# An ordered opening and five rearranged stage borders in a two-block transformer kernel on one Trainium2 core

## The chip, the core and the metric

The kernel runs on one core of a Trainium2 chip. The metric is the device time of one execution in microseconds (us). Times of one execution come from the hardware profiler. Engines are named as the profile names them: PE (TensorE, matrix products; PEld is its weight load), DVE (VectorE), ACT (ScalarE), POOL (GpSimd), SP (SyncE, which issues DMAs). A trailing q (SPq, ACTq) means the queue in which an engine issues.

## The reference

Two transformer blocks work on a batch of one, 512 tokens of width 1024, in fp32. The change touches the first block only:

```
x = x + 0.5 * swiglu(rms_norm(x, norm_ffn1_w), ffn1_w_in, ffn1_w_out)
x = x + hybrid_mixer(rms_norm(x, norm_mix_w), ...)      # SSD scan + differential attention
x = x + memory_cross_attention(rms_norm(x, norm_cross_w), rms_norm(mem, norm_mem_w), w_cq, w_ck, w_cv, w_co)
x = x + 0.5 * swiglu(rms_norm(x, norm_ffn2_w), ffn2_w_in, ffn2_w_out)
...
z, xbc, dt_raw, q, k, v = split_sizes(h @ w_in, IN_SIZES)   # in hybrid_mixer
y = ssd_scan(...) gated by silu(z), normed in 4 groups
logits = q k^T * scale + bias[rel_bucket], causal; w = p0 - lam * p1 ; o = w v, normed per head
return concatenate([y_ssd, y_attn]) @ w_out
```

There are 16 SSD heads of 64 in 4 groups, chunks of 128 tokens, 8 attention heads with two score maps each, a memory of 256 rows with 4 cross-attention heads, and a relative position bias of 32 buckets.

## The kernel before

**Products in three parts.** Every large product is made of fp32r halves: a weight `w` is split into `w_hi` and `w_lo = w - w_hi`, an activation likewise, and `products` (L474 ff.) issues three matmuls, hi·hi (L479), hi·lo (L480) and lo·hi (L481), 128x128 weights by 512 columns each.

**Weights come in units** of 128x1024 (512 KB) through a ring of four slots. SP loads a unit into `w_raw` (first four L408, then L412, each after `unit_lo` says that the slot's last user is split). ACT rounds it to `w_hi` (`round_unit`, L1183; `ahead` rounds the unit three ahead of the one in use), POOL subtracts in four pieces to `w_lo` (L426), PE uses 8 chunks of it (24 matmuls), and `unit_done` counts. One order per engine is written out by hand; the engines meet only in semaphores. A wait that stands first in a queue therefore holds all that is written behind it.

**The opening.** ACT issues the small tables, `cols` (norm weights and others), both halves of x, `consts`, `wdt` and `rows`. PE first makes the position bias sums from `relb` and `onehot` (L689, L690), DVE subtracts them from `pen` (`brow`, L1749), ACT writes `brow` to DRAM (L1289), and then, for each of 8 chunks of x: ACT squares (L1296) and makes `gx_hi` (L1297), DVE adds the square to `sumsq` (L1648) and makes `gx_lo` (L1658). One `square` tile serves all chunks, so ACT and DVE alternate. Once that is through, ACT spreads the bias in DRAM (2.5 MB, L1302). `tiles(..., together=3)` runs ffn1's first three output tiles chunk by chunk, so that PE can begin when chunk 0 is there and the unit's `w_lo` too. Behind the group stand the norm's sums (`stat`, L654), tile 3 with the norm's row (L661) inside, and then the loop.

**Mixer.** Stages run xbc, z (token major, `token_group`, two groups of four weight units, banks 2 to 5), the SSD loop over 16 cells (`ssd_front` L736 ff., `ssd_back`) with q's units between, k, v (two token groups; `turn_y` L788 transposes SSD output between units, in banks 6 and 7), then 8 attention heads. A token group's banks are evacuated on ACT by `token_evac` (L1235), four tiles per group, and counted in `token_free`. A head's step on PE is: three scores (L814), `ssd_part` (a quarter and a quarter of one mix_ssd unit, bank 1), the transposes of the head before (`turn`, L825), five scores, half a unit, the values of the head before (L838). DVE adds bias and takes the minimum (`biased`, L1965), combines both maps (`combine`), copies o (`values_copied`, L1941) and adds the mix_ssd tile to x (L1991); the next `ssd_part` needs that add.

**Memory.** Stage mix_attn follows (8 units, banks rotating over five). Beside each of its tiles ACT and DVE make one tile of the normalized memory (`memory_tile`: square L1418, `m_hi` L1419, sum L2005, `m_lo` L2007). Then ck (memory keys, 256 columns, two banks) with `m_stat` and `m_rows` as hooks in its first two tiles, and cv (memory values, two token groups of two tiles, banks 2 and 3 both times).

## Time and profile before

| | us |
|---|---|
| median of 3 runs | 2224.64 |
| lowest, highest | 2221.55, 2225.09 |
| profiled execution | 2218.06 |
| its span in the trace | 2216.3 |
| PE busy | 2160.7 |
| POOL busy | 1114.0 |
| DVE busy | 828.2 |
| ACT busy | 780.3 |

The span is the part of an execution between the first and the last instruction; 1.8 us lie around it. PE's busy time counts overlapping matmuls as one stretch. The granted TensorE clock was 0.999 of full over the span.

### The profile page before, as it was taken

What the parts mean: (1) busy time and instruction counts of PE and PEld (TensorE: products, weight loads), DVE (VectorE), ACT (ScalarE), POOL (GpSimd) and SP (SyncE); (2) the same over time, 40 slices, a digit from 0 to 9 for tenths busy, and PEclk for the clock granted to TensorE, in tenths of its full rate; (3) what the DMA queues carried; (4) which work ended last, traced back from release to release, by engine and by line L of the source; (5) the groups of instructions that cost most, each with busy time, mean ns of one, the idle gap of its engine ahead of it and who ended that gap; (6) DMA issues with size and microseconds to landing.
All of it is one profiled execution on the core that took longest, in us unless ns stands there. A gap on an engine that the chain in (4) does not pass through costs nothing.

```text
span 2216.3 us, 29399 instructions
## 1 busy us (share of the span) xinstructions
PE 2160.7 (97%) x10276; PEld 1777.1 (80%) x10276; DVE 828.2 (37%) x1502; ACT 780.3 (35%) x1209; POOL 1114.0 (50%) x1493
## 2 busy tenths in 40 slices
PE   7999999999999999999999999999999989999999
PEld 5888888878887677877888888888787878888887
DVE  4222211744831666034222221207743364013234
ACT  4322223225424445323322223325544243212233
POOL 5555555663244225834555556554554456555554
PEclk9999999999999999999999999999999999999999
DMA  6322333231132112512232233222222313322322
GB/s 213 106 95 95 98 110 98 85 100 62 48 97 76 56 48 95 164 65 67 87 101 96 95 104 104 96 93 70 73 80 67 95 58 114 104 96 96 104 86 76
DMA packets 58910, 203.46 MB, mean 92 GB/s; under 512 B 6296, under 2 KB 7704, under 8 KB 58824
## 3 DMA queue, kind: packets, MB, share of 16 engines
q1 hardware_dynamic: 53568, 192.96, 26.8%
q10 hardware_dynamic: 5256, 9.30, 1.2%
q8 instruction: 61, 1.00, 0.2%
q14 instruction: 25, 0.20, 0.0%
HBM read 200.12 MB, written 4.74 MB: 92 GB/s over the span
## 4 chain that ended last, share of the span: by engine, by line
PE 77%; issue 9%; POOL 8%; DVE 4%; ACT 1%; POOLq 0%; DVEq 0%; ACTq 0%
PE bank L479 21%; PE bank L481 20%; PE bank L480 20%; POOL w_lo L426 8%; PE bank L632 2%; PE bank L634 2%; PE bank L633 2%; PE bank L814 1%; PE bank L838 1%; PE bank L741 1%; PE bank L987 1%; PE bank L968 1%; PE bank L750 1%; PE bank L1051 1%; DVE gx_lo L2195 1%
## 5 line engine op out<-in xcount | busy, mean ns | idle before, releaser
L426 POOL TENSOR_TENSOR w_lo<-w_raw,w_hi 128x256 fp32r<-128x256 f32 x1448 | 1080.7, 779 | 1006.3 <-ACT w_hi L1183 1006.1
L479 PE MATMUL bank<-gx_hi,w_hi 128*128 128x512 f32 (+1 forms) x1776 | 683.6, 385 | 20.9 <-DVE gx_lo L1658 5.8
L481 PE MATMUL bank<-gx_hi,w_lo 128*128 128x512 f32 (+1 forms) x1776 | 675.0, 380 | 0.0
L480 PE MATMUL bank<-gx_lo,w_hi 128*128 128x512 f32 (+1 forms) x1776 | 674.5, 380 | 0.0
L1183 ACT CAST w_hi<-w_raw 128x1024 fp32r<-128x1024 f32 x364 | 379.0, 1045 | 361.2 <-PE bank L481 314.5
L479 PEld LDWEIGHTS bank<-gx_hi,w_hi 128*128 128x128 f32 x1776 | 334.1, 188 | 92.1 <-issue 10.0
L481 PEld LDWEIGHTS bank<-gx_hi,w_lo 128*128 128x128 f32 x1776 | 334.2, 188 | 64.1
L480 PEld LDWEIGHTS bank<-gx_lo,w_hi 128*128 128x128 f32 x1776 | 334.4, 188 | 61.9 <-issue 0.2
L479 PE MATMUL bank<-ff_hi,w_hi 128*128 128x512 f32 x352 | 136.9, 389 | 0.0
L480 PE MATMUL bank<-ff_lo,w_hi 128*128 128x512 f32 x352 | 136.9, 389 | 0.0
L481 PE MATMUL bank<-ff_hi,w_lo 128*128 128x512 f32 x352 | 136.9, 389 | 0.0
L479 PE MATMUL bank<-up_hi,w_hi 128*128 128x512 f32 (+1 forms) x288 | 105.4, 366 | 0.0
L480 PE MATMUL bank<-up_lo,w_hi 128*128 128x512 f32 (+1 forms) x288 | 105.2, 365 | 0.0
L481 PE MATMUL bank<-up_hi,w_lo 128*128 128x512 f32 (+1 forms) x288 | 105.2, 365 | 0.0
L1705 DVE TENSOR_TENSOR ff_up<-bank,rstd_row 128x512 f32<-128x512 f32 x44 | 30.4, 690 | 189.9 <-PE bank L481 189.9
L1253 ACT CAST ff_hi<-ff_act 128x512 f32 (+1 forms) x44 | 27.3, 620 | 191.1 <-DVE ff_act L1709 191.1
L479 PEld LDWEIGHTS bank<-ff_hi,w_hi 128*128 128x128 f32 x352 | 66.1, 188 | 13.8
L480 PEld LDWEIGHTS bank<-ff_lo,w_hi 128*128 128x128 f32 x352 | 66.1, 188 | 13.6
L481 PEld LDWEIGHTS bank<-ff_hi,w_lo 128*128 128x128 f32 x352 | 66.1, 188 | 13.6
L1249 ACT ACTIVATE ff_silu<-ff_gate 128x512 f32<-128x512 f32 x44 | 27.8, 632 | 121.5 <-DVE ff_gate L1702 121.5
L632 PE MATMUL bank<-w_hi,gx_hi 128*128 128x512 f32 x160 | 63.6, 398 | 1.9 <-ACT v_tok L1235 1.4
L1702 DVE TENSOR_TENSOR ff_gate<-bank,rstd_row 128x512 f32<-128x512 f32 x44 | 30.4, 691 | 88.6 <-PE bank L481 88.6
(343 smaller groups left out, 2719.8 us busy)
## 6 DMA issues: line engine op xcount, KB each, us to landing
w_raw<-wstream SPq DMA_DIRECT2D x364, 512.0 KB, 3.4
bias_spread<-bias_rows ACTq DMA_DIRECT2D x1, 2560.0 KB
x<-xT ACTq DMA_DIRECT2D x2, 1024.0 KB, 10.4
outT<-ple_o SPq DMA_DIRECT2D x8, 256.0 KB, 2.0
square<-bias_spread ACTq DMA_DIRECT2D x4, 256.0 KB, 2.8
rfin_row<-bias_spread ACTq DMA_DIRECT2D x4, 256.0 KB, 2.7
m_T<-memT ACTq DMA_DIRECT2D x1, 1024.0 KB, 5.4
p_T<-pT ACTq DMA_DIRECT2D x1, 512.0 KB, 4.3
```

The costliest lines, as they stand in the source:

```text
L426: ins = nc.gpsimd.tensor_tensor(w_lo[:, s, part], w_raw[:, s, part], w_hi[:, s, part].bitcast(F32), ALU.subtract)
L479: nc.tensor.matmul(dst, hi, rhs[0], start=first, stop=False)
L480: nc.tensor.matmul(dst, hi, rhs[1], start=False, stop=False)
L481: return nc.tensor.matmul(dst, lo, rhs[0], start=False, stop=last)
L632: nc.tensor.matmul(dst, a[0], rh, start=(k == 0), stop=False, skip_group_check=True)
L633: nc.tensor.matmul(dst, a[1], rh, start=False, stop=False, skip_group_check=True)
L634: mm = nc.tensor.matmul(dst, a[0], rl, start=False, stop=(k == DC - 1), skip_group_check=True)
L1183: nc.scalar.copy(w_hi[:, j, :], w_raw[:, j, :]).then_inc(unit_hi, 1)
L1249: nc.scalar.activation(ff_silu[:, :], ff_gate[:, :], ACT.Silu).then_inc(sem("ffn_silu"), 1)
L1253: nc.scalar.copy(tile_of(ff_hi, c), ff_act[:, :]).then_inc(sem("ffn_act_hi"), 1)
L1702: nc.vector.tensor_tensor(ff_gate[:, :], bank[2 * j][:, :], rstd_row[:, :], ALU.mult)\
L1705: nc.vector.tensor_tensor(ff_up[:, :], bank[2 * j + 1][:, :], rstd_row[:, :], ALU.mult)\
```

## The change

Six things, all in the first block.

1. **Opening.** SP interleaves the weight units with three quarters of x; ACT loads only `cols` and the first quarter of x. ACT makes all of `gx_hi` before any square; the squares go to eight tiles of their own (`load_sq`), and DVE makes all of `gx_lo` before the sums. On PE, `opening_group` replaces the chunk-by-chunk group: first the hi·hi and hi·lo matmuls of all chunks (these need `w_hi` only), then the 24 lo·hi matmuls. The bias sums (`brow_sums`) move behind tile 3, DVE's `bias_rows` and ACT's `spread_bias` behind the second ffn1 column.
2. **SSD.** The cumulative sums are matmuls inside z's second group (u = 6), the three exponentials of the decays stand before z's last evacuation, and the SSD loop waits for z's evacuated tiles one by one.
3. **v groups.** `turn_y` uses bank 7 only, and v's second group takes banks 0, 6, 2, 3.
4. **Heads, first.** Head 0 begins with half a mix_ssd unit (four of its eight chunks), and its scores wait for two evacuated tiles instead of four.
5. **Heads, each.** DVE adds the mix_ssd tile to x before it copies o.
6. **Memory.** `memory_tile` runs three tiles ahead of mix_attn (three of them before its first tile); `m_stat` moves behind mix_attn's tile 6, `m_rows` before ck; cv's groups take banks 2, 3 and 4, 5.

```diff
@@ sync
             for s in range(RING):
                 sp.dma_start(w_raw[:, s, :], wstream[s]).then_inc(unit_raw[s], 16)
+                if s < 3:
+                    sp.dma_start(x[:, 2 * s + 2:2 * s + 4, :], x_d[:, 2 * s + 2:2 * s + 4, :])\
+                      .then_inc(sem(f"x_in{s + 1}"), 16)
...
@@ tensor
+            def opening_group():
...
+                for k in range(DC):
+                    arrived(k)
+                    if k == 3:
+                        for kk in range(3):
+                            high(2, kk)
+                    for j in range(3 if k > 2 else 2):
+                        high(j, k)
+                for j in range(3):
+                    pe.wait_ge(unit_lo, j + 1)
...
-            ffn("ffn1", "n_ffn1", "load")
+            ffn("ffn1", "n_ffn1", "load", hooks=(((3, 7), brow_sums),), opening=opening_group)
...
+                if n < 2:
+                    pe.wait_ge(sem("token_free"), 5 + n)
...
-            pe.wait_ge(sem("token_free"), 8)
...
-            for g in range(2):
-                token_group("v", g, (gx_hi, gx_lo), TT, 8 + 4 * g, between=turn_y)
-            pe.wait_ge(sem("token_free"), 16)
+            token_group("v", 0, (gx_hi, gx_lo), TT, 8, between=turn_y)
             pe.wait_ge(tile_free, TILE0["mix_ssd"])
+            token_group("v", 1, (gx_hi, gx_lo), TT, 12, order_of=V_BANKS, between=turn_y, freed=(0, 0, 9, 10))
...
             for h in range(AH):
+                if h == 0:
+                    ssd_part(h, range(0, 4))
+                    pe.wait_ge(sem("token_free"), 14)
...
+                if j == 6:
+                    m_stat()
+            m_rows()
...
@@ scalar
-            act.wait_ge(sem("brow_out"), 16)
-            act.dma_start(bias_t, ...).then_inc(sem("bias_spread"), 16)
+            def spread_bias():
+                act.wait_ge(sem("brow_ready"), 2)
+                act.dma_start(bias_r, brow[0:AH, :]).then_inc(sem("brow_out"), 16)
+                act.wait_ge(sem("brow_out"), 16)
+                act.dma_start(bias_t, ...).then_inc(sem("bias_spread"), 16)
...
-            residual_stage("mix_attn", "norm_cross_w", 1, body=8, peel=1, beside=memory_tile)
+            for m in range(3):
+                memory_tile(m)
+            residual_stage("mix_attn", "norm_cross_w", 1, body=8, peel=1, beside=memory_beside)
...
@@ vector
-                if h > 0:
-                    values_copied(h - 1)
                 dve.wait_ge(unit_done, UNIT0["mix_ssd"] + h + 1)
                 nc.vector.tensor_tensor(x[:, h, :], bank[1][:, :], x[:, h, :], ALU.add).then_inc(tile_free, 1)
+                if h > 0:
+                    values_copied(h - 1)
```

PE at the beginning of head 0, before. `k_T,q_T` are scores, `ys_hi` and `ys_lo` the SSD output that a mix_ssd unit multiplies, `z_tok` the last transposes of `turn_y`.

```order
L788 MATMUL bank<-consts,z_tok 128x128 x4
L814 MATMUL bank<-k_T,q_T 128x128 x2
L814 MATMUL bank<-k_T,q_T 128x256
L479 MATMUL bank<-ys_hi,w_hi 128x512
L480 MATMUL bank<-ys_lo,w_hi 128x512
L481 MATMUL bank<-ys_hi,w_lo 128x512
```

And after:

```order
L832 MATMUL bank<-consts,z_tok 128x128 x4
L491 MATMUL bank<-ys_hi,w_hi 128x512
L492 MATMUL bank<-ys_lo,w_hi 128x512
L493 MATMUL bank<-ys_hi,w_lo 128x512
...
L859 MATMUL bank<-k_T,q_T 128x128 x2
L859 MATMUL bank<-k_T,q_T 128x256 x2
L859 MATMUL bank<-k_T,q_T 128x384 x2
L859 MATMUL bank<-k_T,q_T 128x512 x2
```

Twelve matmuls of the unit moved ahead of the scores, and all eight scores of head 0 now stand in a row.

ACT at the beginning of stage mix_attn, before. `o_hi` is the last head's output, `w_hi` a weight unit, `m_sq` and `m_hi` a memory tile.

```order
L1388 CAST o_hi<-o_nrm 128x512
L1183 CAST w_hi<-w_raw 128x1024
L1206 ACTIVATE square<-x 128x512
L1207 ACTIVATE gx_hi<-x,cols 128x512
L1418 ACTIVATE m_sq<-m_T 128x256
L1419 ACTIVATE m_hi<-m_T,cols 128x256
L1183 CAST w_hi<-w_raw 128x1024
```

And after:

```order
L1444 CAST o_hi<-o_nrm 128x512
L1474 ACTIVATE m_sq<-m_T 128x256
L1475 ACTIVATE m_hi<-m_T,cols 128x256
L1474 ACTIVATE m_sq<-m_T 128x256
L1475 ACTIVATE m_hi<-m_T,cols 128x256
L1474 ACTIVATE m_sq<-m_T 128x256
L1475 ACTIVATE m_hi<-m_T,cols 128x256
L1238 CAST w_hi<-w_raw 128x1024
L1261 ACTIVATE square<-x 128x512
```

Three memory tiles, each with a wait for DVE's running sum, now stand ahead of the rounding of mix_attn's unit 3.

DVE at the end of a head's step, before. `w_T` and `o_un` are copies of the transposed weights and of the head's values, `prob` the next head's first biased score.

```order
L1937 COPY w_T<-bank 128x384
L1930 TENSOR_TENSOR o_lo<-o_nrm,o_hi 128x512
L1941 COPY o_un<-bank 128x512
L1991 TENSOR_TENSOR x<-bank,x 128x512
L1965 ISA prob,amin<-bank,rfin_row 128x128
```

And after:

```order
L2009 COPY w_T<-bank 128x384
L2002 TENSOR_TENSOR o_lo<-o_nrm,o_hi 128x512
L2061 TENSOR_TENSOR x<-bank,x 128x512
L2013 COPY o_un<-bank 128x512
L2037 ISA prob,amin<-bank,rfin_row 128x128
```

The add, which waits for a unit that PE finishes before the head's values, changed places with the copy of those values.

## Rows read from the trace of the kernel before

**Rows 1.** The page, busy time of each engine and share of the span.

```profile
PE 2160.7 (97%) x10276; PEld 1777.1 (80%) x10276; DVE 828.2 (37%) x1502; ACT 780.3 (35%) x1209; POOL 1114.0 (50%) x1493
```

**Rows 2.** Waits of PE: line, releaser, us in total, times, longest.

```profile
PE bank L479 <- DVE x L1991: 3.7, 6, 0.6
```

**Rows 3.** Timeline of PE, opening: start, duration, line, count, idle before.

```profile
9.18 1.87 PE L689 MATMUL bank<-onehot,relb 32*8 32x512 f32 x2 [9.18 <-DMA cols<-cols]
10.85 0.63 PE L690 MATMUL bank<-onehot,relb 32*8 32x128 f32 x2
16.32 0.76 PE L479 MATMUL bank<-gx_hi,w_hi 128*128 128x512 f32 x1 [4.84 <-DVE gx_lo L1658]
...
20.28 0.50 PE L479 MATMUL bank<-gx_hi,w_hi 128*128 128x512 f32 x1 [1.06 <-POOL w_lo L426]
...
35.39 0.95 PE L654 MATMUL bank<-consts,sumsq 128*128 128x1 f32 x8
```

**Rows 4.** Timelines of ACT, POOL and DVE, opening.

```profile
13.68 0.71 ACT L1297 ACTIVATE gx_hi<-x,cols 128x512 fp32r<-128x512 f32 x1
...
9.72 10.51 POOL L426 TENSOR_TENSOR w_lo<-w_raw,w_hi 128x256 fp32r<-128x256 f32 x12 [8.88 <-ACT w_hi L1183]
...
15.01 1.21 DVE L1658 SCALAR_TENSOR_TENSOR gx_lo<-x,cols,gx_hi 128x512 fp32r<-128x512 f32 x1
```

**Rows 5.** Stretches of the opening: busy by engine, granted clock, DMA share, GB/s.

```profile
4.00:6.00 2.00, 0.00 (x0) 0.00 (x0) 0.00 (x0) 0.00 (x0) 0.00 (x0) 1.00 1.04 371
```

**Rows 6.** DMA issues of the first 40 us: count, size, median us to landing.

```profile
x<-xT ACTq DMA_DIRECT2D x2, 1024.0 KB, 10.4
```

**Rows 7.** Timelines at the SSD and v borders, DVE and PE.

```profile
523.06 0.69 DVE L1804 COPY xs_tok<-bank 128x512 f32<-128x512 f32 x1 [5.23 <-PE bank L710]
...
525.19 0.46 PE L736 MATMUL bank<-bc 128*128 128x128 f32 x2 [1.77 <-ACT z_tok L1235]
...
684.26 0.47 PE L632 MATMUL bank<-w_hi,gx_hi 128*128 128x512 f32 x1 [1.45 <-ACT v_tok L1235]
```

**Rows 8.** Timeline of PE at the beginning of head 0.

```profile
707.61 0.60 PE L788 MATMUL bank<-consts,z_tok 128*128 128x128 f32 x4
711.30 0.98 PE L814 MATMUL bank<-k_T,q_T 64*128 64x128 f32 x6 [3.09 <-ACT v_tok L1235]
712.21 0.79 PE L479 MATMUL bank<-ys_hi,w_hi 128*128 128x512 f32 x1
...
716.64 2.82 PE L814 MATMUL bank<-k_T,q_T 64*128 64x256 f32 x10
```

**Rows 9.** Timeline of DVE there, the first biased score.

```profile
713.25 0.29 DVE L1965 CUSTOM_DVE_ANT_0 prob<-bank,square 128x128 f32<-128x128 f32 x1
```

**Rows 10.** Timelines of ACT, DVE and POOL in stage mix_attn.

```profile
845.43 1.05 ACT L1183 CAST w_hi<-w_raw 128x1024 fp32r<-128x1024 f32 x1
...
850.81 0.40 ACT L1418 ACTIVATE m_sq<-m_T 128x256 f32<-128x256 f32 x1
...
846.26 0.27 DVE L2000 MEMSET m_sum<- 128x256 f32 x1
...
851.61 0.42 DVE L2005 TENSOR_TENSOR m_sum<-m_sum,m_sq 128x256 f32<-128x256 f32 x1
...
852.63 4.59 POOL L426 TENSOR_TENSOR w_lo<-w_raw,w_hi 128x256 fp32r<-128x256 f32 x5 [3.25 <-ACT w_hi L1183]
```

**Rows 11.** Timeline of PE in mix_attn, ck and cv.

```profile
850.09 0.39 PE L479 MATMUL bank<-o_hi,w_hi 128*128 128x512 f32 x1
...
856.40 0.50 PE L479 MATMUL bank<-o_hi,w_hi 128*128 128x512 f32 x1 [0.71 <-POOL w_lo L426]
...
883.60 0.38 PE L479 MATMUL bank<-m_hi,w_hi 128*128 128x256 f32 x1 [2.64 <-DVE m_lo L2007]
...
889.25 0.39 PE L479 MATMUL bank<-m_hi,w_hi 128*128 128x256 f32 x1 [1.27 <-DVE kx_T L1687]
...
918.55 0.47 PE L632 MATMUL bank<-w_hi,m_hi 128*128 128x512 f32 x1 [0.87 <-ACT vx L1235]
```

## What the change does to the time

> **What bounds the kernel now.** The page's first part comes first: PE is busy for 97% of the span [rows 1], so a microsecond counts only where PE stands still or runs slowly. The list of PE's waits and its timeline then show where. The opening has 16.3 us before the first product, a slow stretch and another pause [rows 3]; the other pauses are 0.6 to 3.1 us at stage borders [rows 2, 7, 8, 11]. After each of them PE runs on without a gap, so what is saved at one border should stay saved. The timelines of ACT, DVE and POOL there tell what PE waited for. The granted clock stands at 1.00 even in the opening [rows 5]; TensorE's two levels, 1.2 and 2.4 GHz, are read from the matmuls instead: 0.79 or 0.76 us at the low level against 0.39 to 0.50 at the high one [rows 3, 8, 11]. The low level shows in two places: from 16.3 until just before 20.3 us, and from 712.2 on, after an idle of 3.09.
>
> **1. Opening.** Before, the group of three units is 72 matmuls: six at the low level, then 66 from 20.28 to 35.39 [rows 3], which is 0.229 us each. After, I follow the arrivals. The DMA engines move 371 GB/s [rows 5], 0.524 MB per piece in 1.4 us, from about 2 us on. ACT's queue needs only 0.6 MB for `cols` and the first quarter of x, beside SP's unit 0: both are in at 5 to 6 us. Then each further piece comes 1.4 later: unit 1 at about 8, unit 2 at 11, the last quarter at 12.3. ACT: rounding 1.0 per unit [rows 10], `gx_hi` 0.7 [rows 4]. DVE: `gx_lo` 1.2 each while POOL splits beside it (1.21; POOL 10.51 for 12 pieces, 3.5 per unit) [rows 4]. That gives `gx_lo` 0 at 8, 3 at 12.1, 7 at 17, and `w_lo` of unit 2 at 16.6. PE: 10 hi·hi and hi·lo matmuls until 12.6, at half speed; chunk 3's twelve then wait for nothing and end at 15.3 at full speed; the remaining 24 and the 24 with `w_lo` follow, all operands there: 15.3 + 48 x 0.229 = 26.3. The group thus ends near 26.3, not 35.39: **-9.1**. Bounds: the clock rises at 10.5 (25.7) or only at 16.3 as before (28.3).
>
> Behind it, DVE's eight sums (0.7, or 1.2 beside POOL) end at about 23.6, before the norm needs them; unit 3 is split at 23.5. The bias sums no longer stand in idle time: 1.87 and 0.63 at the low clock [rows 3] become 1.2 at the high one, on the path: **+1.2** (0 to 2.5). The two subtractions on DVE and the DRAM round trip on ACT now stand ahead of the rounding of unit 7. The second column is finished when PE begins unit 5, so PE wants unit 7 two units later, 2 x 24 x 0.229 = 11 us; rounding and split take 1.05 + 3.0 (four pieces of 0.75, POOL's mean of 1114.0 over 1493) [rows 1, 10], so a round trip of up to some 5 us costs nothing. Its landing is not in the trace: from below nothing, from above the 10.4 us of x in the full opening [rows 6], which would cost 5. I take 2 to 3 us, nothing, since one weight unit at most moves beside it. The Trainium skill (DMA: Bandwidth & Descriptors, the two cost components of a DMA) names about 2.0 us fixed per DMA; by it the sum stays as it is. Opening: -7.9.
>
> **2. SSD.** PE waited 1.77 us until 525.19 for z's last tile. Now it waits for DVE's last `xs_tok` copy, 523.06 + 0.69 [rows 7], plus 0.3 for the cumulative sums now inside z: start near 524.1, **-1.1**. The table switches move to where ACT waits anyway; the first decay has 3 us of slack under q's twelve matmuls.
>
> **3. v border.** The pause of 1.45 [rows 7] and its restart go, since banks 0 and 6 are free: **-1.6**.
>
> **4. Head 0.** Before: turn at 707.61, idle until 711.30, then twelve chunk matmuls from 712.21 to 716.64 = 4.43 instead of 2.8, then five scores in 2.8 [rows 8]. After: the twelve run at once, 708.1 to 710.95, the first three scores until 711.9. But score 3 needs DVE's first biased tile, and that still comes at 713.25 + 0.29 [rows 9], for DVE waits for lambda's exponential, which stands behind v's evacuation on ACT. So a new wait of 1.6 stands in the place of the 3.09. Gain: 3.1 idle + 1.6 slow clock - 1.6 = **-3.2** (-1.7 if the clock falls all the same).
>
> **5. Heads 2 to 7.** DVE's add is ready during the values on PE: six waits, 3.7 in total [rows 2], go. Everything else on DVE comes 0.6 earlier with it. **-3.6**.
>
> **6. Memory, the gain.** ck's two pauses, 2.64 and 1.27 [rows 11], go, with about 0.5 of restart: memory is three tiles ahead, and `m_rows` has all of tile 7 (5.5 us) to be made ready. **-4.4**. cv's second group takes free banks: 0.87 and its restart, **-1.0** [rows 11].
>
> **7. Memory, the price.** Before, ACT rounded mix_attn's unit 3 at 845.43 at once [rows 10]; PE began on it at 850.09 [rows 11]. Now three memory tiles stand ahead, the first behind DVE's `m_sum` at 846.26, each a square and a sum, 0.40 + 0.42 [rows 10] with two handoffs, 0.9 each: the rounding starts at 849.1, POOL at 850.2. Split beside DVE it takes 0.92 a piece (4.59 for five), against its mean of 0.75 [rows 1, 10]: PE starts at 853.0 to 854.0. Loss 3.3, less the 0.8 that unit 4 lost before (856.40 against 850.09 + 24 x 0.229), which now goes: **+2.5** (+2.0 to +3.1). The idle is about 3.2. One of 3.09 was followed by the low clock [rows 8], one of 2.64 was not (0.38 at 883.60) [rows 11], so I take the fall and its price of head 0: **+1.5** (0 to 1.6). The Trainium skill (TensorE: Matmul & The Clock Gate, Part 1) says that idleness halves the clock and that the point of change differs from run to run; it supports both outcomes at such an idle.
>
> **Sum:** -7.9 - 1.1 - 1.6 - 3.2 - 3.6 - 4.4 - 1.0 + 2.5 + 1.5 = **-18.8**. On the profiled execution (2218.06, span 2216.3) that is 2199.3; on the median of the runs shown, which lies 6.6 above it, 2224.64 - 18.8 = **2205.8**. I forecast 2206.
>
> **The rivals.**
> *No fall of the clock in mix_attn:* the idle stays on the side of the 2.64. 2204.
> *The opening is later:* unit 1 or the first quarter of x comes 2 us later because the queues share otherwise than I assume, or the clock rises at 16.3. For it: before, x on ACT's queue took 10.4 us [rows 6]; against it: 2 MB stood ahead of and beside it then, now 0.6. About +2.5: 2208.
> *The heads' wait is replaced:* the add comes early, but the transposes then wait for DVE's combine. For it: they follow closely on it; against it: the combine moves forward too. +3.6: 2209.
> *Head 0 goes slow as well:* five scores with pauses between them are little work after an idle of 1.6. +1.5: 2207.
> *POOL is shut out:* in mix_attn DVE and POOL take turns by whole instructions. Four pieces of 0.75 with a DVE operation of 0.7 between each would be 5.8 instead of 3.7, +2.1: 2208. Against it, 4.59 for five pieces [rows 10], DVE being as busy. The Trainium skill (SBUF — State Buffer, the shared port pair) states such an exclusive lock.
> *Slower than before:* the DRAM round trip of `brow` holds ACT, and with it the rounding of units 7 and up. It costs its length less 5 us, plus 1.5 for the clock, and eats the 18.8 only from 22 us on, twice what x took in the full opening [rows 6]. 2227 and more; nothing in the trace speaks for it.
>
> **How the numbers follow.** Forecast 0.48 (2203 to 2209); no fall 0.20; later opening 0.12; heads replaced 0.07; head 0 slow 0.06; POOL shut out 0.04; slower 0.02; 0.01 for a change that does little. The bounds above and the runs' own spread of 3.5 us give 2200 to 2212 for eight in ten. A measurement of this kernel tells about 0.2% (4.4 us) from no change; all cases but the last two lie 15 us below, so faster 0.96, same 0.02, slower 0.02.
>
> **What would show it.** The norm's first matmul near 26 us; SSD's first at the old time less 9; no pause at v's border; scores 0 to 2 of head 0 right behind twelve chunk matmuls, then a pause of 1.6 before the fourth; heads 2 to 7 each 0.6 shorter; a new pause of about 3.2 before mix_attn's unit 3 with POOL as releaser, slow matmuls behind it; none in ck and cv. The forecast is wrong if a pause appears in the first ffn loop (rounding of unit 7), or if the new pause in mix_attn is missing (2202).

## The result, and the profile after

| us | before | after |
|---|---|---|
| median | 2224.57 (4 runs) | 2207.28 (4 runs) |
| lowest, highest | 2221.55, 2225.09 | 2206.34, 2208.11 |
| profiled execution | 2218.06 | 2208.11 |
| span, mean granted clock of it | 2216.3, 0.999 | 2206.3, 0.996 |

The ratio of the medians is 0.993 (95% interval 0.9916 to 0.9944): faster by 17.3 us, against a forecast of 18.6 (2206, range 2200 to 2212). Between the two profiled executions, however, only 10.0 us lie, and the same sum had given 2199.3 for the one after. So the median was met and the profiled execution missed by 8.8. Of 41 ordinary executions of before that ran beside the variants below, 12 took 2218 to 2222 us at a mean clock of 0.999, and 29 took 2222 to 2230 us at 0.995 to 0.997. The experiments are mostly about the missed 8.8.

The page of the kernel after, its busy row [rows 1 is the one before]:

```profile
PE 2164.3 (98%) x10276; PEld 1780.9 (81%) x10276; DVE 829.8 (38%) x1502; ACT 781.0 (35%) x1209; POOL 1117.7 (51%) x1493
```

PE is busy 3.6 us more than before although it has the same work. With the same matmuls, a busy time that grows points to more of them at the low level; the timelines below show where.

What PE waits for after the change (us in total, times, longest):

```profile
PE bank L706 <- DVE gx_lo L1720: 10.5, 1, 10.5
PE bank L491 <- POOL w_lo L438: 5.8, 3, 3.8
...
PE bank L491 <- DVE up_t L2324: 2.4, 1, 2.4
PE bank L859 <- DVE amin L2037: 1.8, 1, 1.8
```

The six waits for x [rows 2] are gone, so are those of v's border and of ck and cv. The longest of the waits on `w_lo` (3.8) is the new one in mix_attn, the one on `amin` the new one in head 0.

The opening after, PE and then ACT (start, duration, line, operation, idle time before and its releaser), to be compared with [rows 3, 4]:

```profile
10.45 0.79 PE L706 MATMUL bank<-gx_hi,w_hi 128*128 128x512 f32 x1 [10.45 <-DVE gx_lo L1720]
11.04 0.63 PE L707 MATMUL bank<-gx_lo,w_hi 128*128 128x512 f32 x1
...
14.86 0.40 PE L706 MATMUL bank<-gx_hi,w_hi 128*128 128x512 f32 x1
...
28.94 0.95 PE L670 MATMUL bank<-consts,sumsq 128*128 128x1 f32 x8
```

```profile
4.88 1.05 ACT L1238 CAST w_hi<-w_raw 128x1024 fp32r<-128x1024 f32 x1 [1.92 <-DMA w_raw<-wstream]
8.78 1.34 ACT L1340 ACTIVATE gx_hi<-x,cols 128x512 fp32r<-128x512 f32 x2 [2.85 <-DMA x<-xT]
```

From 10.45 on PE has no gap in the opening. Products are slow (0.63) until 14.86 and fast (0.39) behind that. The group starts late because the first quarter of x does: ACT waits for it until 8.78.

Head 0 after, PE and DVE, to be compared with [rows 8, 9]:

```profile
703.24 0.92 PE L859 MATMUL bank<-k_T,q_T 64*128 64x128 f32 x6
705.95 3.85 PE L859 MATMUL bank<-k_T,q_T 64*128 64x256 f32 x10 [1.79 <-DVE amin L2037]
709.73 0.79 PE L491 MATMUL bank<-ys_hi,w_hi 128*128 128x512 f32 x1
...
714.16 0.58 PE L492 MATMUL bank<-ys_lo,w_hi 128*128 128x512 f32 x1
```

```profile
705.60 0.29 DVE L2037 CUSTOM_DVE_ANT_0 prob<-bank,square 128x128 f32<-128x128 f32 x1
```

The pause of 1.79 is where and as long as foreseen (1.6). But the five scores behind it take 3.85, not 2.82 [rows 8], and the products behind them run at the low level up to 714.16.

Stage mix_attn after, ACT, POOL and PE, to be compared with [rows 10, 11]:

```profile
835.07 0.42 ACT L1474 ACTIVATE m_sq<-m_T 128x256 f32<-128x256 f32 x1 [1.09 <-DVE m_sum L2072]
...
837.62 1.04 ACT L1238 CAST w_hi<-w_raw 128x1024 fp32r<-128x1024 f32 x1
```

```profile
838.74 6.81 POOL L438 TENSOR_TENSOR w_lo<-w_raw,w_hi 128x256 fp32r<-128x256 f32 x8 [8.01 <-ACT w_hi L1238]
```

```profile
842.48 0.80 PE L491 MATMUL bank<-o_hi,w_hi 128*128 128x512 f32 x1 [3.78 <-POOL w_lo L438]
```

ACT's rounding stands behind the three memory tiles, POOL's split waits for the rounding, and PE waits for the split.

In the second block, where the code is the same, PE after the wait for `up_t`:

```profile
1817.34 0.77 PE L491 MATMUL bank<-gx_hi,w_hi 128*128 128x512 f32 x1 [2.42 <-DVE up_t L2324]
```

The same pause was 2.38 long before, but there no low clock followed it (0.47 and then 0.39 a matmul). This costs the profiled execution 1.5 us.

### The profile page after: what moved, and what is told of

It reads as the page before. It is cut to its first block, busy times and chain, and to the rows that moved or that the text cites. A ratio compares the mean times of both kernels' runs of the same rounds, so it can differ in the third digit from the quotient of the medians.

```text
span 2206.3 us, 29404 instructions
## 1 busy us (share of the span) xinstructions
PE 2164.3 (98%) x10276; PEld 1780.9 (81%) x10276; DVE 829.8 (38%) x1502; ACT 781.0 (35%) x1209; POOL 1117.7 (51%) x1493
## 4 chain that ended last, share of the span: by engine, by line
PE 79%; issue 9%; POOL 8%; DVE 3%; ACT 1%; DMA 0%; POOLq 0%; ACTq 0%; DVEq 0%
PE bank L491 21%; PE bank L493 21%; PE bank L492 21%; POOL w_lo L438 8%; PE bank L648 2%; PE bank L650 2%; PE bank L649 2%; PE bank L859 1%; PE bank L883 1%; PE bank L784 1%; PE bank L1042 1%; PE bank L1023 1%; PE bank L795 1%; PE bank L1106 1%; DVE gx_lo L2273 1%
## 5 line engine op out<-in xcount | busy, mean ns | idle before, releaser
L491 PE MATMUL bank<-gx_hi,w_hi 128*128 128x512 f32 (+1 forms) x1752 | 674.4, 385 | 15.1 <-DVE gx_lo L2273 4.1
L493 PE MATMUL bank<-gx_hi,w_lo 128*128 128x512 f32 (+1 forms) x1752 | 665.6, 380 | 0.0
L492 PE MATMUL bank<-gx_lo,w_hi 128*128 128x512 f32 (+1 forms) x1752 | 665.1, 380 | 0.0
L493 PEld LDWEIGHTS bank<-gx_hi,w_lo 128*128 128x128 f32 x1752 | 329.6, 188 | 63.2
```

Source lines behind the costliest of these rows:

```text
L491: nc.tensor.matmul(dst, hi, rhs[0], start=first, stop=False)
L492: nc.tensor.matmul(dst, hi, rhs[1], start=False, stop=False)
L493: return nc.tensor.matmul(dst, lo, rhs[0], start=False, stop=last)
```

## The experiments

All variants compute the whole reference. Times are medians of 4 to 12 executions. The kernel before, run beside them, had 2223.0, 2223.4 and 2222.2 in the three groups of runs, and the last column is a ratio to that (with its 95% interval). "Rounded first" means that ACT rounds a unit of mix_attn ahead of the memory tiles; the three mends together are x and `gx_hi` first, units 3 and 4 rounded first, and lambda late.

| kernel | median | lowest, highest | against before |
|---|---|---|---|
| before, again | 2223.97 | 2219.88, 2225.08 | 1.0003 |
| heads alone | 2220.28 | 2217.66, 2223.63 | 0.9984 [0.9974, 0.9994] |
| after | 2207.28 | 2206.34, 2208.11 | 0.993 [0.9916, 0.9944] |
| unit 3 rounded first | 2209.36 | 2205.75, 2210.10 | 0.9938 [0.9925, 0.9952] |
| memory part undone | 2209.07 | 2206.10, 2211.20 | 0.994 [0.9927, 0.9954] |
| head 0, scores first | 2205.99 | 2205.74, 2207.42 | 0.9929 [0.9915, 0.9942] |
| x first | 2205.72 | 2204.79, 2207.37 | 0.9927 [0.9913, 0.994] |
| x and `gx_hi` first | 2205.17 | 2204.51, 2206.72 | 0.9916 [0.9904, 0.9929] |
| lambda late | 2204.19 | 2203.57, 2204.43 | 0.9917 [0.9903, 0.993] |
| units 3 and 4 rounded first | 2203.56 | 2202.20, 2204.83 | 0.991 [0.9897, 0.9923] |
| three mends, two taken further | 2202.49 | 2201.90, 2203.95 | 0.9913 [0.9899, 0.9926] |
| three mends together | 2200.27 | 2198.71, 2201.28 | 0.9893 [0.9878, 0.9907] |

### The kernel before, again and a third time

> The kernel before, unchanged. Its profiled execution took 2218.06 us, 6.6 below the median of its ordinary runs (2224.64); the change's profiled execution, 2208.11, lies at its own median (2207.28). So trace against trace gives 10.0 us and median against median 17.3. Theory A (the pauses in which the clock falls differ from one execution to the next): a second profile shows low-clock stretches at pauses where the first had none, and is longer by 1.5 us for each, around 2224. Theory B (the profiler or the launch accounts for it): the second profile shows the same low-clock stretches as the first and the same 2218, with the ordinary runs at 2224.

> The kernel before once more, for its trace. Its executions fall in two groups: 2218 to 2221 at a mean granted clock of 0.999, and 2222 to 2226 at 0.995 to 0.997. Both profiled ones so far are of the first group and show one low stretch behind the opening (head 0, seven products of 0.63). Theory A (the slower group has one or two more low stretches at pauses that the two groups share): if this profiled execution lies above 2222, it shows a low stretch at the up_t pause near 1829, or at another pause, that the other two don't, of 1.5 to 2.5 us each. If it lies at 2218 to 2221 it shows none and tells nothing new.

The second profiled execution (2219.88) has the same low stretches as the first, only that in the opening 15 products are slow and not 6, which is all of the 1.8 us between them. So far theory B was still open. The third took 2224.7 us at a mean clock of 0.996. Its timeline at ck, where the first had 0.38 at 883.60 [rows 11]:

```profile
885.91 0.58 PE L479 MATMUL bank<-m_hi,w_hi 128*128 128x256 f32 x1 [2.63 <-DVE m_lo L2007]
886.30 0.41 PE L480 MATMUL bank<-m_lo,w_hi 128*128 128x256 f32 x1
```

The clock column of two stretches, the first execution and then the third (stretch, its length, busy time and instructions of PE, PEld, DVE, ACT, POOL, granted clock, DMA share, GB/s):

```profile
880.00:892.00 12.00, 8.09 (x67) 7.70 (x66) 4.45 (x8) 6.28 (x9) 8.32 (x12) 1.00 0.26 91
1780.00:1800.00 20.00, 16.34 (x123) 14.89 (x122) 17.96 (x36) 10.86 (x25) 16.84 (x23) 1.00 0.29 100
```

```profile
880.00:892.00 12.00, 9.37 (x53) 9.05 (x52) 5.33 (x10) 6.51 (x10) 6.49 (x9) 0.74 0.27 87
1780.00:1800.00 20.00, 18.03 (x125) 17.62 (x125) 14.97 (x31) 11.41 (x25) 15.99 (x22) 0.84 0.33 106
```

Measured by how late the same matmul comes, the third execution loses 2.3 us to the first in the opening (18 slow products instead of 6), 2.9 at ck and 1.3 near 1790 to 1800; the rest of its 6.6 is 0.1. So theory A holds and B falls: an execution under the profiler can be as long as the ordinary ones, and its extra time lies in low stretches. The pauses are others than I had named: `up_t` is not among them, and the stretch near 1790 stands behind pauses of only 1.07 and 0.90 us, at which the first execution kept its clock. Part of this goes with the change, because it removes ck's pause. The profiled execution of before, on which the forecast's terms were read, was a lucky one.

### The heads alone

```diff
+                dve.wait_ge(unit_done, UNIT0["mix_ssd"] + h + 1)
+                nc.vector.tensor_tensor(x[:, h, :], bank[1][:, :], x[:, h, :], ALU.add).then_inc(tile_free, 1)
                 if h > 0:
                     values_copied(h - 1)
-                dve.wait_ge(unit_done, UNIT0["mix_ssd"] + h + 1)
-                nc.vector.tensor_tensor(x[:, h, :], ...).then_inc(tile_free, 1)
```

> The kernel before, with one part of the change alone: DVE's add to x ahead of the copy of the previous head's values. Theory A (each of PE's six waits of 0.6 for x goes and nothing takes its place): heads 2 to 7 each 0.6 to 0.7 shorter, 3.6 to 4.1 in total, no wait for x left: 3.6 to 4.1 below the kernel before, runs of equal clock compared. Rival B (part of the gain was due to the other parts of the change, the earlier chunks of head 0 above all): under 2.5.

From head 1 to head 7 PE gains 4.0 us on the first trace of before (its lead moves from -3.3 to +0.7, 0.7 a head), and no wait for x is left. By the traces this is theory A. The medians differ by 3.1, a little less than its 3.6, and the lowest runs by 2.1; none of the 12 executions reached the mean clock of 0.999 that before has in some. In its trace the clock fell at ck and behind `up_t`, where the first trace of before kept it, 1.5 us each. Whether the edit has to do with that is not shown.

### Head 0: lambda late, and the scores first

Lambda late moves DVE's wait for lambda behind the first three biased scores:

```diff
-            dve.wait_ge(sem("lam_exp"), 1)
-            link(nc.vector.tensor_tensor(lam[:, 4:5], ...))
-            link(nc.vector.tensor_scalar(lam[:, 5:6], ...))
...
                 for n in range(3):
                     biased(h, n)
+                if h == 0:
+                    dve.wait_ge(sem("lam_exp"), 1)
+                    link(...); link(...)
```

> The change, with DVE's two operations on lambda (and its wait for ACT's exponential) moved from ahead of head 0's biased scores to ahead of head 0's combine. Theory A (the 1.79 us pause of PE after score 2 is DVE waiting for lambda's exponential, and the clock falls on it): DVE's first biased score comes at about 703.9 and not at 705.6, the pause shrinks to 0.2 to 0.5, head 0's five scores take 2.8 to 3.0 and not 3.85, head 1's chunk products run at 0.39 and not at 0.63 to 0.79: gain 1.6 for the pause, 0.9 for the scores and 2.6 for the chunks, some 3 to 5 us, median 2203 (2202 to 2205). Rival B (the clock falls here whatever the pause, since scores are light work): the pause goes but the chunks still run at 0.63: 2205.7. Rival C (ACT's table load and exponential hold the first exponentials of the scores, so DVE's later operations wait): the whole moves by under 0.5 us: 2207.

PE in lambda late:

```profile
703.23 2.48 PE L859 MATMUL bank<-k_T,q_T 64*128 64x128 f32 x12
706.00 1.60 PE L859 MATMUL bank<-k_T,q_T 64*128 64x512 f32 x4 [0.29 <-DVE amin L2034]
707.53 0.50 PE L491 MATMUL bank<-ys_hi,w_hi 128*128 128x512 f32 x1
```

The pause is 0.29, no product behind it is slow, and head 0 is 4.4 us shorter than in the trace of after. The median, 2204.19, is 3.1 below that of after and in the range of theory A; the profiled execution has two low stretches elsewhere (14 slow products in mix_attn, and one near 1773). The five executions lie within 0.9 us of each other, the narrowest of all the variants.

The other run gives PE its old order back for head 0 and leaves the rest changed:

```diff
                 if h == 0:
-                    ssd_part(h, range(0, 4))
                     pe.wait_ge(sem("token_free"), 14)
                 for n in range(3):
                     score(h, n // 2, n % 2)
-                if h > 0:
-                    ssd_part(h, range(0, 2))
+                ssd_part(h, range(0, 2))
...
-                if h > 0:
-                    ssd_part(h, range(2, 4))
+                ssd_part(h, range(2, 4))
```

> The change with head 0's order on PE as before: scores 0 to 2 ahead of the twelve chunk products, all else as changed. Theory A (the reordering gains 3.0 us where the clock holds, as in two of the traces of this order, and about nothing where it falls): the scores wait 1.9 for v's last evictions and then nothing waits for lambda, since the chunks stand between; head 0 takes 1 to 3 us longer than with the chunks first and a held clock: 2208 (2207 to 2209.5). Rival B (the new order's pause of 1.8 behind the scores costs as much as the old order's pause, and the clock falls at both): 2207, no difference.

```profile
702.76 0.92 PE L859 MATMUL bank<-k_T,q_T 64*128 64x128 f32 x6 [1.93 <-ACT v_tok L1287]
703.61 0.50 PE L491 MATMUL bank<-ys_hi,w_hi 128*128 128x512 f32 x1
...
706.55 2.82 PE L859 MATMUL bank<-k_T,q_T 64*128 64x256 f32 x10
```

Theory A falls: this variant is not slower than the change, but 1.3 lower by the medians, with overlapping runs. Rival B, no difference, is nearer, but its reason falls too, for in this trace the clock did not fall at all. Now the wait is 1.93, not the 3.09 of before, because v's second group is evicted in another order, and twelve long products follow it at full speed. The three traces of the change's order in which the clock held (x first, unit 3 rounded first, memory part undone) show what the reordering itself brings: from the first transpose of `turn_y` in the window of head 0 to the first of `turn(0)` they take 21.8 us, scores first takes 22.05. In the three where it fell (after, units 3 and 4 first, x and `gx_hi` first) it is 24.7 to 25.0, and with lambda late 20.6. So the reordering gains 0.25 or loses 2.7 to 2.9. (Scores first has one trace; whether its clock falls in other executions is not shown.)

### The opening: x first, then `gx_hi` first

```diff
# x first
+            sp.dma_start(x[:, 0:2, :], x_d[:, 0:2, :]).then_inc(sem("x_in0"), 16)
             for s in range(RING):
                 sp.dma_start(w_raw[:, s, :], wstream[s]).then_inc(unit_raw[s], 16)
...
-            act.dma_start(x[:, 0:2, :], ...).then_inc(sem("x_in0"), 16)
# x and gx_hi first, as well
-            round_unit(0, 0)
             act.wait_ge(sem("cols_in"), 16)
...
-                if m in (1, 3):
-                    round_unit(m // 2 + 1, m // 2 + 1)
+                if m == 1:
+                    round_unit(0, 0)
+                    round_unit(1, 1)
+                if m == 3:
+                    round_unit(2, 2)
```

> The change, with the first quarter of x issued by SP ahead of weight unit 0; ACT's queue keeps cols alone. Theory A (the quarter came at 8.7 us and not at 5 to 6 because ACT's queue got a small share of the DMA engines beside SP's): it lands by about 5 us, the first product starts near 7.8 us and not at 10.45, and the norm's first product moves from 28.94 to about 26.3 (the forecast's number), 2.6 us less: median 2204.7. Rival B (the end of the group hangs on the last arrivals, unit 2's w_lo and the last gx_lo, not on its start): a pause opens inside the group and its end moves by under 1 us: 2206.5 to 2207.3. Rival C (the clock rises a fixed time after the end of the start-up, not 4.4 us after the first product): more products run at 0.63 us and half the gain is lost: 2206.

> The change, with the first quarter of x ahead of weight unit 0 on SP's queue, and on ACT the two gx_hi of that quarter ahead of the rounding of unit 0. With the queue's order alone changed (x_first), the quarter landed 5.4 us into the span, not 8.7, but ACT waited for unit 0 until 6.8 and rounded it first, so the first product came at 9.95 instead of 10.45; the fast products began at 15.15, not 14.86. Theory A (the end of the group follows its start): gx_hi 0 at 5.5, first product at about 7.9, fast products 4.5 to 5 us later, the norm's first product near 26.8 (28.94 in the change): median 2205.2. Rival B (the clock rises near 15 us whatever the start): seven more products run at 0.63 us, which gains half: norm near 27.7, 2206. Rival C (POOL's split of unit 2 or DVE's low parts come too late): a pause opens in the group and its end moves by less than 0.5 us.

ACT and PE in x first:

```profile
6.82 1.04 ACT L1239 CAST w_hi<-w_raw 128x1024 fp32r<-128x1024 f32 x1 [4.33 <-DMA w_raw<-wstream]
7.77 1.33 ACT L1340 ACTIVATE gx_hi<-x,cols 128x512 fp32r<-128x512 f32 x2
```

```profile
9.95 0.79 PE L707 MATMUL bank<-gx_hi,w_hi 128*128 128x512 f32 x1 [9.95 <-DVE gx_lo L1720]
```

The quarter of x landed 4.7 us after its issue (7.5 on ACT's queue), but now the weight unit came at 6.8 and ACT rounded it first. So the landing is that of theory A, but the first product comes only 0.5 earlier and the norm's first one, at 28.77, only 0.2: no theory is met. The trace gives the opening 0.2 us of the median's 1.6; of the 3.3 between the two profiled executions 3.2 are head 0, where the clock held this time. In the other variant ACT meets its table load, which waits for x as well:

```profile
5.63 1.28 ACT L1339 ACT_TABLE_LOAD   x1 [5.63 <-DMA x<-xT]
6.92 1.33 ACT L1339 ACTIVATE gx_hi<-x,cols 128x512 fp32r<-128x512 f32 x2
```

PE starts at 9.34, 1.1 before that of after, and the norm's first product stands at 27.87, 1.1 earlier as well. So the end follows the start, as theory A says, and the start missed its 7.9 by the table load. Rival B falls, for the fast products begin at 13.2 and not near 15. Neither variant reached the 26.8 or 26.3 expected.

### mix_attn: the roundings first, the memory part undone

```diff
# unit 3 rounded first
+            ahead("mix_attn", 0, 8, 0)
             for m in range(3):
                 memory_tile(m)
-            residual_stage("mix_attn", ..., beside=memory_beside)
+            residual_stage("mix_attn", ..., beside=memory_beside, rounded=1)   # no ahead for tile 0
# units 3 and 4 rounded first: behind memory_tile(m), as well
+            ahead("mix_attn", 0, 8, 1)
-            residual_stage("mix_attn", ..., beside=memory_beside)
+            residual_stage("mix_attn", ..., beside=memory_beside, rounded=2)   # no ahead for tiles 0, 1
```

> The change, with ACT rounding weight unit 3 of stage mix_attn ahead of the three memory tiles, not behind them. Theory A (the new pause of 3.78 us with POOL's w_lo as releaser is the rounding that stands behind the memory tiles, and the low clock follows the pause): ACT rounds near 834 us, not at 837.6, POOL's split ends before PE needs it, the pause falls under 0.5 us, no matmul of 0.63 or 0.80 us behind it, and the shift of mix_attn's last unit against the kernel before goes from -5.9 to about -11; median 2207.3 - 5 = 2202 (2201 to 2204). Rival B (POOL is shut out by DVE's memory tiles, whenever it is given the unit): it starts earlier but ends hardly earlier, the pause stays over 2 us, median 2206 to 2207. Rival C (the memory tiles now come 1 us later and ck waits again): the pause goes but ck shows a pause of 0.5 to 1 us, 2203.

> The change, with ACT rounding unit 3 of mix_attn ahead of the three memory tiles and unit 4 right behind them, ahead of its operations on the first x tile (the roundings of all later units move forward by one tile too). With unit 3 alone moved (mix_round), the pause of 3.78 before unit 3 went and one of 3.07 stood before unit 4, whose rounding waited behind ACT's square of x, which waited for DVE's x tile 0 at 837.4, which stood behind DVE's six memory operations, 0.95 us each beside POOL. Theory A (that chain is the only cause): unit 4 is rounded near 836.3, split by 840, and no pause is left before units 3 and 4, with no low clock behind it: mix_attn ends 5 us earlier than in the change, median 2202.3 (2201 to 2203.5). Rival B (POOL beside DVE cannot keep up with PE in this stage at all: 3.4 us per unit beside DVE's load, so pauses only move on to units 5 and 6): mix_attn ends 3 us or less earlier, 2204 to 2205.

PE, and then ACT and DVE, with unit 3 alone moved:

```profile
844.74 0.50 PE L491 MATMUL bank<-o_hi,w_hi 128*128 128x512 f32 x1 [3.07 <-POOL w_lo L438]
```

```profile
838.02 0.63 ACT L1261 ACTIVATE square<-x 128x512 f32<-128x512 f32 x1 [1.88 <-DVE x L1733]
...
839.88 1.03 ACT L1238 CAST w_hi<-w_raw 128x1024 fp32r<-128x1024 f32 x1
```

```profile
834.34 0.95 DVE L2079 TENSOR_TENSOR m_sum<-m_sum,m_sq 128x256 f32<-128x256 f32 x1
835.22 0.96 DVE L2081 SCALAR_TENSOR_TENSOR m_lo<-m_T,cols,m_hi 128x256 fp32r<-128x256 f32 x1
```

The pause before unit 3 is gone (PE is 9.0 us ahead of the trace of after at the unit's end, 2.5 of it since the clock held in head 0), and one of 3.07 stands before unit 4 with the low clock behind it. The chain is longer than I had seen: DVE's memory tiles, three of whose six operations now run beside POOL at 0.95 instead of 0.42 to 0.49, hold its add to x; ACT's square waits for that add; the rounding of unit 4 stands behind the square. None of the three theories had this. The median is 2 us above that of the change; the two executions with a mean clock of 0.998 took 2205.8 and 2206.1, the three with 0.995 took 2209.4 to 2210.1. The trace does not explain the 2 us: it is one of the two, its mix_attn is 1.5 us shorter than that of after, and a low stretch at 1409, behind a pause of 0.96, takes 1.6 back. What the other three lost, and where, stays open. With unit 4 moved as well, no pause stands before units 3 and 4, one of 2.0 before unit 5 is left, and mix_attn is 4.2 us shorter than in the trace of after. The median is 3.7 below the change: between theories A and B.

> The change with its memory part alone undone: the memory tiles beside the residual tiles again, m_stat and m_rows within ck; cv's banks stay as changed. Left out of the change: three tiles ahead of the rounding of unit 3. By the traces that part took 5.1 us off ck's pauses and put 5.6 on mix_attn. Theory A (the part is worth nothing, gain and price cancel): ck's pauses of 2.6 and 1.3 come back, the pause of 3.78 before unit 3 falls to 0, one of 0.7 before unit 4 is back, and the low clock in mix_attn goes: 2206.8, within 1.5 of the change's 2207.3. Rival B (part of the price is due to the shorter heads, which bring unit 3's want forward): a pause of 1 to 2 us stays before unit 3, 2208 to 2209. Rival C (the 5.1 of ck was mostly the new banks and not the order of tiles): the time falls to 2203.

```profile
869.14 0.58 PE L491 MATMUL bank<-m_hi,w_hi 128*128 128x256 f32 x1 [2.64 <-DVE m_lo L2071]
869.51 0.41 PE L492 MATMUL bank<-m_lo,w_hi 128*128 128x256 f32 x1
```

(In the diff of this run the three hunks on `memory_beside`, `m_stat` and `m_rows` are those of the change, backwards.) mix_attn has no pause before unit 3 and 0.71 before unit 4; ck's 2.64 and 1.3 are back, this time with the low clock. By the traces the price in mix_attn is 5.5 to 5.6, the gain in ck 4.4 where the clock would have held and 7.3 where it would have fallen. No pause of 1 to 2 us stays before unit 3, so rival B's mechanism falls, though its number is the one that came; the time did not fall to 2203, so rival C falls. The shape is that of theory A, but its 2206.8 was missed by 2.3: in the profiled execution the clock fell at ck (2.8), and again in a stretch at 1412, behind a pause of 0.96 (1.6). The median is 1.8 above the change's with overlapping runs (2206.1 to 2211.2 against 2206.3 to 2208.1), so the memory part is worth about 2 us by the medians. By the traces it loses 1.1 where ck's clock would have held (4.4 against 5.5) and gains 1.8 where it would have fallen.

### The mends together

> The change with all three edits together: the opening of open2, the roundings of mix_round2, lambda late as in lam_late. Theory (the gains are independent, since PE has no other pause between): 1.5 to 2 for the opening, 5 for mix_attn, 3 to 4 for head 0 against the change's 2207.3: median 2197.5 (2196 to 2199.5). Rival (the clock falls at one of the pauses that are left, the up_t pause of 2.4 us in the second block above all, more often when the others go): 2199 to 2201.

> As all3, with two mends. ACT: a copy of one column ahead of everything, so that the load of its table (1.28 us, which in open2 stood between the landing of x at 5.6 and gx_hi at 6.9) lies in the wait for the data; and the roundings of mix_attn one more tile early, each behind the memory tile of the block before the last. Theory A (the table load and the rounding behind ACT's wait for DVE's x tile are the next terms): first product near 8.1 (9.33 in all3), norm's first product 1.2 earlier; POOL's pause of 2.0 before unit 5 and the low clock behind it go, 3.3 less: median 2200.3 - 4.5 = 2195.8 (2195 to 2197.5). Rival B (POOL beside DVE is slower than PE's unit, 6.85 for two units with 3.4 a unit against PE's 5.5, so nothing is late for long): holds with A. Rival C (ACT waits for PE's unit in the middle of a block and so holds the x tile): a pause moves to cq or ck, 2198.

Together the three mends give 2200.27, 23 us below before. They are additive within 2 us: 2.1 + 3.7 + 3.1 = 8.9 by their own medians, 7.0 together. That is 2.8 above the 2197.5 of the theory and inside the rival's range; in the trace the clock fell behind unit 5's pause of 1.95 and behind `up_t`, but the latter it did in the trace of after too, so "more often" is not shown. The further mends of the last variant (ACT's table loaded while it waits for data, and mix_attn's roundings another tile early) made it 2.2 slower. Its PE, in the opening and in mix_attn, and then at the start of the second block:

```profile
8.04 0.76 PE L707 MATMUL bank<-gx_hi,w_hi 128*128 128x512 f32 x1 [8.04 <-DVE gx_lo L1728]
8.60 0.63 PE L708 MATMUL bank<-gx_lo,w_hi 128*128 128x512 f32 x1
10.47 0.79 PE L707 MATMUL bank<-gx_hi,w_hi 128*128 128x512 f32 x1 [1.24 <-ACT w_hi L1239]
...
857.22 0.61 PE L967 MATMUL bank<-consts,m_sum 128*128 128x1 f32 x4 [1.11 <-DVE m_sum L2086]
...
865.06 0.71 PE L974 MATMUL bank<-consts,m_rstd 128*128 128x128 f32 x4 [1.66 <-DVE m_rstd L2096]
...
1402.62 0.50 PE L492 MATMUL bank<-gx_hi,w_hi 128*128 128x512 f32 x1 [0.95 <-DVE gx_lo L1728]
...
1405.95 0.63 PE L493 MATMUL bank<-gx_lo,w_hi 128*128 128x512 f32 x1
```

PE starts at 8.04 as expected, but after two products unit 1 is late (idle 1.24), and products stay slow until 15.7: the norm's first one comes at 28.87, later than with the start at 9.33 (28.26). In mix_attn POOL's pause is gone, and two waits on DVE's `m_sum` and `m_rstd` stand further on. This is rival C's shape, a stage earlier than it said. Against the trace of the three mends the opening loses 0.6 and mix_attn gains 0.6. The 1.6 us between the two profiled executions are the last two lines, a low stretch behind a pause of 0.95 at which the clock held before. Whether the 2.2 of the medians are such stretches too is not shown.

## Why the prediction came out as it did

Lead of PE over before, read at the same matmul in the two profiled executions:

| step | forecast | traces | what the runs add |
|---|---|---|---|
| opening group | -9.1 | -6.5 | -7.9 between means of 4 and 6 traces |
| bias sums on the path | +1.2 | +1.3 | |
| cumulative sums and SSD | -1.1 | -0.8 | |
| v border | -1.6 | -1.7 | |
| head 0 | -3.2 | +0.2 | -3.0 where the clock held |
| heads 2 to 7 | -3.6 | -4.1 | -4.0 alone |
| mix_attn, new pause and clock | +4.0 | +5.6 | 5.5 against the memory part undone |
| ck | -4.4 | -4.4 | -7.3 where the clock falls in ck |
| cv | -1.0 | -1.1 | |
| second block | 0 | +1.5 | clock behind `up_t`: fell in 9 of 10 traces with the change, 1 of 4 without |
| sum | -18.8 | -10.0 | medians -17.3 |

**Opening: mechanism right, size wrong.** The step that failed is "both are in at 5 to 6 us"; it is the rival of the later opening that came true. I divided bytes by the full rate from 2 us on; weight unit 0 was in by 4.9, but the quarter of x on ACT's queue took 7.5 us beside SP's queue, and at the head of SP's it took 4.7. By 8.7 us some 2.4 MB had moved (DMA rates of about 400 GB/s from 3 us on), so ACT's queue had got a quarter of it. The length of the slow stretch differs from trace to trace besides. The "full speed from 20.28" of [rows 3] was the best of four: the norm's first product came at 35.39, 37.20 and 37.75 in the three traces of before and at 37.30 in the heads alone, which has the same opening; in six kernels with the changed opening it came at 28.5 to 29.6. The working also counted 10, 12 and 48 matmuls, 70 of the group's 72, which is 0.5 us too few.

**Head 0: the pause right, its effect wrong.** The wait of 1.79 came as worked out. I charged it the idle time alone and gave the low clock behind it a rival of 0.06; it fell in three of six traces of that order. The term also credited the reordering with what the evictions' order brings: without the reordering the kernel is as fast. (Its own numbers, 3.1 + 1.6 - 1.6, add up to 3.1 and not 3.2.)

**mix_attn: the right rows, a price too small.** The rounding at 837.62 and the splits at 838.74 are those foreseen (849.1 and 850.2 of old time, less the 11.5 of lead). PE began at the late end of the range, 3.9 lost instead of 3.3, and the low clock over twelve products cost 2.6 with the restart, not the 1.5 of head 0; unit 4 gave back 1.0, of which 0.7 is its own old pause. That the clock would fall was right: it fell in all five traces with this pause. The POOL rival's 2.1 us did not come: eight pieces took 6.81, as they took 6.86 in before. That DVE and POOL take turns is not refuted by it (see the last section); only two of unit 3's four pieces met an operation of DVE that slowed them (1.19 and 1.17, the other two 0.73).

**Heads, ck, cv, v, SSD, bias sums:** each within 0.5 us. No pause appeared in the first ffn loop, so the DRAM round trip cost nothing.

**Why the sum still met the median.** The terms missed by +8.8 on the profiled execution. The base missed by about as much the other way: I took the 6.6 between the profiled execution and the median of before as a constant to be added on both sides. It was low clock, in the opening and at ck among others, and the change removes ck's pause. After, the profiled execution is not below the median but 0.8 above it, so the base was 7.4 too high. Two errors cancelled. The forecast was right in its sign and its number, but the number was met partly by luck, for nothing in the working makes +8.8 and -7.4 cancel. For ck (3 falls in 5 traces) and for the opening the low clock of before is seen more than once; the stretch near 1790 was slow in one of before's three traces, and also in that of lambda late, so its share stays open. Open too is `up_t`: its code and its pause are the same in all kernels, yet in before's three traces the clock held, and with the change it fell in 9 of 10. The one exception, lambda late, had the low stretch just ahead of it. Four traces without the change are too few to say whether these 1.5 us are a price of the change.

## What to carry to other kernels

Before terms are summed against one profiled execution, ask whether that execution had the mean granted clock of ordinary ones; a gap between it and the median is not a constant that a change leaves alone. Price a pause with the slow matmuls that can follow it, here 1.5 to 2.9 us each time. Compare traces stretch by stretch before a difference of medians is put down to an edit: several of 1.5 us lay in code that the edit had not touched. When work is put ahead of a weight's rounding, follow the roundings of the next two units as well, through every engine that the in-order queue of the rounding one waits for.

## What the runs showed of the hardware

The clock behind one and the same pause, counted over the 14 traces (fell: matmuls of 0.63, or 0.41 at 256 columns, the 1.2 GHz level, at once or within 3 us behind it):

| pause of PE | idle, us | fell |
|---|---|---|
| mix_attn, unit 3 | 3.8 | 5 of 5 |
| head 0, old order and evictions | 3.1 | 4 of 4 |
| mix_attn, unit 4 (unit 3 rounded first) | 3.1 | 1 of 1 |
| ck | 2.6 | 3 of 5 |
| second block, `up_t` | 2.4 | 10 of 14 |
| mix_attn, unit 5 (two variants) | 2.0 | 1 of 2 |
| head 0, scores first, new evictions | 1.9 | 0 of 1 |
| head 0, new order, then scores | 1.8 | 3 of 6 |
| SSD's first, before | 1.8 | 0 of 4 |
| second block, first product on `o_hi` | 1.7 | 0 of 14 |
| second block, near 1790, two pauses | 1.1, 0.9 | 2 of 14 |
| start of the second block, near 1410 | 1.0 | 3 of 14 |
| head 0, lambda late | 0.3 | 0 of 3 |

At idle times between 0.9 and 2.6 us the same code held the clock in one trace and lost it in another. The length of the pause alone does not decide: 1.7 never lost it in 14 traces, 1.0 did in three. Nor does it help to have long products behind the pause and not light ones, as far as these rows show: long ones follow the 1.7, but also the 2.4, and the light ones behind SSD's 1.8 kept the clock as well.

The slow stretch after the first product lasted 3.2 to 9.2 us in the 14 traces, and in the three of before it had 6, 15 and 18 slow products. The Trainium skill (TensorE: Matmul & The Clock Gate, Part 1) says that the point of change differs from run to run; these traces agree.

In the opening the profile's clock column read 1.00 while matmuls took 0.63, so there it must be read from the matmuls.

In mix_attn an operation of DVE of 0.42 alone took 0.95 beside POOL's splits. I had weighed only what POOL loses by that. The rows of before's opening show how the two meet, DVE and then POOL:

```profile
18.43 1.22 DVE L1648 TENSOR_TENSOR sumsq<-sumsq,square 128x512 f32<-128x512 f32 x1
19.57 1.21 DVE L1658 SCALAR_TENSOR_TENSOR gx_lo<-x,cols,gx_hi 128x512 fp32r<-128x512 f32 x1
20.70 0.68 DVE L1648 TENSOR_TENSOR sumsq<-sumsq,square 128x512 f32<-128x512 f32 x1
```

```profile
19.06 1.17 POOL L426 TENSOR_TENSOR w_lo<-w_raw,w_hi 128x256 fp32r<-128x256 f32 x1
```

From 14.5 to 20.2 both engines start an operation every 1.14 us, each in the middle of the other's; alone DVE takes 0.68 and a piece of POOL 0.72. Beside DVE's operations of 256 columns (in the trace of unit 3 rounded first, from 833.4 on) the two start every 0.88 us. DVE's add of a bank to x took 0.63 to 0.69 beside POOL's splits in mix_attn, no more than without them. In these rows the two engines' start times alternate, as they would if the engines took turns; a mean over a stage hides it.
